# Attention in a two-layer hybrid encoder: the scores of three pairs of heads change their slot

## The chip, the cores and the metric

One core of a Trainium2 chip runs the whole program. The metric is device time in microseconds of one execution. The kernel before took 1118.52 us (median of 3 runs, 1117.92 to 1119.52). All times below come from these runs or from the trace of one profiled execution.

## The reference

Input x is 256 tokens by 1024 channels in float32. Each of two layers does

```
x = LN(alpha*x + 0.5*SwiGLU_1(x))
x = LN(alpha*x + HybridMixer(x))
x = LN(alpha*x + 0.5*SwiGLU_2(x))
```

The mixer multiplies x by one combined input matrix. Its columns feed a state-space branch (u), an indexer (idx), attention (q, k, v; 8 heads of 64) and two gates (gs, ga). The state-space branch is a complex diagonal recurrence per group of 16 channels, then GELU and a gated linear unit. The attention branch lets each query keep its 64 best keys as scored by the indexer, adds a relative-position bias, takes a softmax and multiplies by v:

```
logits = q @ k * HEAD_DIM**-0.5 + bias[bucket(key - query)]   (selected keys only)
p = softmax(logits); out = p @ v
merged = sigmoid(g_ssm)*(y_ssm @ w_branch[0]) + sigmoid(g_attn)*(y_attn @ w_branch[1])
return merged @ w_out
```

## The kernel before, in words

Every weight arrives in tiles of 128 partitions by up to 1024 columns. SyncE loads a tile into a ring of four raw buffers, ScalarE rounds it into a high part (`whi`, `split_hi`, L430), VectorE subtracts to get the low part (`wlo`, `split_lo`, L1246), and TensorE multiplies three times (high by high, high by low, low by high: L744 to L746). A raw buffer is free once its tile is split, so each load waits for the split of four tiles earlier. Each of the five engines runs its own instruction list in order; the lists meet only through semaphores.

In the mixer TensorE runs nine projections c = 0 to 8, each for two token tiles t, each in four quarters q of two contraction tiles (six matmuls a quarter at 512 columns). Small work of the other branches is hooked in after a quarter. Attention is hooked into projections 6 to 8; the quarters there are slots j = 8*(c-6) + 4*t + q, from 0 to 23. The weights of a projection's quarter q are one tile; tiles 20 to 23 belong to projection 7, tiles 24 to 27 to projection 8, tiles 28 and 29 to the gated linear unit, and tiles 30 to 33 to the product after it (counted as in `splits(s + n)`).

The heads go in four pairs p. A pair passes through these steps:

- `att_scores` (TensorE, L1038, 64 rows of the array each): q times k on top of a mask that lies in banks 4 and 2 of PSUM. For pairs 1 to 3 ScalarE has to have put the mask there (`set_masks`, L594).
- `att_logits` (VectorE, L1457): adds the bias, writes `prob` and the negative maximum. From pair 1 on it also waits until the transposes of the pair before have read `prob`.
- `exp_probs` (ScalarE, L584), `invert` (VectorE, L1466), `normalize` (ScalarE, L612).
- `prob_transpose` (TensorE, L1049): turns the probabilities. It waits for `normalize` and for `ya_lo` of the pair before.
- `prt_read` (ScalarE, L602): copies them to SBUF.
- `att_values` (TensorE, L1059, 64 columns of the array each): multiplies by v.
- `ya_hi` (ScalarE, L617) and `ya_lo` (VectorE, L1470): split the output into two parts.

In the same slots the state-space branch has `ssm_out` (TensorE, L999 and L1004), `ssm_turn` and `ssm_scan` (VectorE, L1398 to L1413) and `rotate_back` (GpSimd, L1840 and following). ScalarE also reads the gate projections out of PSUM (`proj_read`, L520). The order in each engine's list is written by hand as a loop over j with tables of slots. Before the change scores stand at slots 3, 7, 11, 15, transposes at 7, 11, 15, 19, values at 8, 12, 16 and 22; in a shared slot the scores come first. `ssm_out` 1 to 3 stand after slots 1, 12 and 17.

VectorE's list from slot 7 on reads: logits of pair 1, split of tile 23, `invert` 1, `ya_lo` 0, `ssm_turn` 3, `ssm_scan` 3, logits of pair 2, split 24, `invert` 2, split 25, `ya_lo` 1, logits of pair 3, split 26, `invert` 3, `ya_lo` 2, split 27. ScalarE's list after the exponentials of pair 1 reads: `ya_hi` 0, `normalize` 1, masks, `proj_read(6,1)`, split 24.

Of the kernel before, what the change touches and what calls it, by code (L numbers as in the profile page):

```python
# [73 lines left out]
TURN_AT = [(1, 1, 1), (2, 0, 1)]  # L74
TURNED = {2: 0, 3: 6}
IDX_AT = [(2, 1, 1), (2, 1, 3), (3, 0, 2)]
OUT_AT = [(5, 1, 1), (6, 0, 1), (7, 1, 1), (8, 0, 1)]
ATT_C = 6
SCORES_AT, TRANSPOSE_AT, VALUES_AT = 3, 7, 8
LAST_VALUES_AT = 22  # L80
GATE_TILES = {1: 22, 2: 23, 8: 24, 13: 27, 16: 28, 17: 29, 18: 30, 20: 31, 21: 32, 22: 33, 23: 34}
READ_AT = {4: (6, 0), 8: (6, 1), 12: (7, 0), 17: (7, 1), 20: (8, 0), 23: (8, 1)}
SLOTS = 8 * (NPROJ - ATT_C)
LAST_K = 3
# [6 lines left out]
N_PAIRS = N_HEADS // 2  # L91
# [10 lines left out]
def build(nc, A, out):  # L102
# [217 lines left out]
    with block:  # L320
# [102 lines left out]
        def _(act):  # L423
# [191 lines left out]
            def ya_hi(l, p):  # L615
                act.wait_ge(S["pv_done"], N_PAIRS * l + p + 1)
                nc.scalar.copy(ya_h[:, p, :], ps[:, PV, 0:SEQ]).then_inc(S["yah_done"], 1)  # L617
# [5 lines left out]
            def mixer(l):  # L623
# [35 lines left out]
                    nc.scalar.copy(y_h[:, cols, :], u_t[:, cols, :]).then_inc(S["yh_done"], 1)  # L659

                for j in range(SLOTS):
                    p, rest = divmod(j - TRANSPOSE_AT, 4)
                    if rest == 0 and 0 <= p < N_PAIRS:
                        prt_read(l, p)
                    if j == 11:
                        splits(s + 25, 2)
                    p, rest = divmod(j - SCORES_AT, 4)
                    if rest == 0 and 0 <= p < N_PAIRS:
                        exp_probs(l, p)
                    if rest == 1 and 1 <= p < N_PAIRS:  # L670
                        ya_hi(l, p - 1)
                    if j == LAST_VALUES_AT:
                        ya_hi(l, N_PAIRS - 1)
                    if rest == 1 and 0 <= p < N_PAIRS:
                        normalize(l, p)
                        if p + 1 < N_PAIRS:
                            set_masks()
                        else:
                            load_table(ACT.Gelu_apprx_tanh)
                    if j in READ_AT:  # L680
                        proj_read(l, *READ_AT[j])
                    if j in GATE_TILES:
                        splits(s + GATE_TILES[j], 1)
                    if j == 18:
                        gelu(0)
                        gelu(1)
                splits(s + 35, 1)
# [53 lines left out]
        def _(pe):  # L741
# [319 lines left out]
                ins.then_inc(S["pv_done"], 1)  # L1061

            def attention(l, j):
                p, last = divmod(j - SCORES_AT, 4)
                if last == 0 and 0 <= p < N_PAIRS:
                    att_scores(l, p)
                p, last = divmod(j - TRANSPOSE_AT, 4)
                if last == 0 and 0 <= p < N_PAIRS:
                    prob_transpose(l, p)
                p, last = divmod(j - VALUES_AT, 4)  # L1070
                if j == LAST_VALUES_AT:
                    att_values(l, N_PAIRS - 1)
                if last == 0 and 0 <= p < N_PAIRS - 1:
                    att_values(l, p)

            def hooks(l, c, t, q):

                for n, where in enumerate(TURN_AT):
                    if (c, t, q) == where:
                        proj_transpose(l, n)  # L1080
                for half, where in enumerate(PAIR_IN):
                    if (c, t, q) == where:
                        ssm_in(l, half)
                for n, where in enumerate(IDX_AT):
                    if (c, t, q) == where:
                        idx_scores(l, n)
                for n, where in enumerate(OUT_AT):
                    if (c, t, q) == where:
                        ssm_out(l, n)
                j = 8 * (c - ATT_C) + 4 * t + q  # L1090
                if j >= 0:
                    attention(l, j)

            def gate_product(l):

# [124 lines left out]
            for l in range(DEPTH):  # L1220
# [4 lines left out]
                last = l + 1 == DEPTH  # L1225
# [3 lines left out]
        def _(dve):  # L1229
# [243 lines left out]
            def mixer(l):  # L1473
# [24 lines left out]
                                                   op0=ALU.add, op1=ALU.mult).then_inc(S["bra_read"], 1)  # L1498

                for j in range(SLOTS):  # L1500
                    p, rest = divmod(j - SCORES_AT, 4)
                    if j == 0:
                        ssm_turn(l, 2)
                    if j == 2:
                        ssm_scan(l, 2)
                    if rest == 0 and 0 <= p < N_PAIRS:
                        att_logits(l, p)
                    if j == 3:
                        splits(s + 20, 1)
                        invert(l, 0)  # L1510
                        splits(s + 21, 2)
                    if j == 7:
                        splits(s + 23, 1)
                        invert(l, 1)
                        ya_lo(l, 0)
                        ssm_turn(l, 3)
                    if j == 10:
                        ssm_scan(l, 3)
                    if j == 11:
                        splits(s + 24, 1)  # L1520
                        invert(l, 2)
                        splits(s + 25, 1)
                        ya_lo(l, 1)
                    if j == 15:
                        splits(s + 26, 1)
                        invert(l, 3)
                        ya_lo(l, 2)
                        splits(s + 27, 1)
# [415 lines left out]
```

## Time and profile before

| what | value |
|---|---|
| median of 3 runs | 1118.52 us |
| lowest and highest | 1117.92 and 1119.52 us |
| span of the profiled execution | 1117.5 us |
| TensorE busy | 1105.8 us, 99% |
| VectorE busy | 752.0 us, 67% |
| ScalarE busy | 561.1 us, 50% |
| GpSimd busy | 391.1 us, 35% |
| granted clock of TensorE, mean | 0.999 |

The profiled execution gives a span from its first to its last instruction, 1117.5 us; what lies around that span is seen only as the difference to the runs, 1.0 us to their median. Matmuls overlap by a pipeline, so that one of 0.39 us starts every 0.23 us; distances between starts are more telling than durations. The attention slots of the first layer lie at about 272 to 320 us of the span, those of the second at about 825 to 872 us.

### The profile page before, as it was taken

The page shows a single profiled execution, that of the slowest core. Times are in us where ns is not written, and L with a number is a line of the kernel's source. Part 1 is how long each engine was busy: PE and PEld are TensorE (multiplying, and loading weights), DVE is VectorE, ACT ScalarE, POOL GpSimd, SP SyncE. Part 2 cuts the span into 40 slices and gives each one's busy share as a digit, 9 for nine tenths or more (in the row PEclk, how much of TensorE's full clock was granted, in tenths as well). Part 3 has the DMA queues.
Part 4 walks back from the last instruction along what each step waited for, and adds up shares of the span by engine and source line. Part 5 has one row for each costly group of instructions (what it writes and reads, how often), then busy time and mean ns, then how long its engine had stood idle before and what let it go on. Part 6 is the DMA issues. An engine that isn't in the chain of part 4 may idle for free.

```text
span 1117.5 us, 17726 instructions
## 1 busy us (share of the span) xinstructions
PE 1105.8 (99%) x5979; PEld 917.9 (82%) x5979; DVE 752.0 (67%) x1073; ACT 561.1 (50%) x805; POOL 391.1 (35%) x560
## 2 busy tenths in 40 slices
PE   9999999999999999999999999999999999999997
PEld 7788888997788888888888888889877888888886
DVE  6657755789977865675575555467898787565544
ACT  6545433674873554543344544336748645453540
POOL 4889975107700188998500000011275000000001
PEclk9999999999999999999999999999999999999999
DMA  9776753644565577565367575536535666657541
GB/s 287 242 228 208 247 176 113 211 136 137 157 223 192 166 224 242 184 221 187 112 201 227 159 245 192 192 91 226 164 112 160 209 199 210 211 172 241 189 150 38
DMA packets 158655, 208.95 MB, mean 187 GB/s; under 512 B 12760, under 2 KB 107128, under 8 KB 158592
## 3 DMA queue, kind: packets, MB, share of 16 engines
q1 hardware_dynamic: 155232, 202.29, 56.7%
q10 hardware_dynamic: 2592, 3.67, 1.2%
q0 software_dynamic: 768, 2.17, 0.6%
q8 instruction: 37, 0.61, 0.2%
q14 instruction: 26, 0.21, 0.1%
HBM read 207.02 MB, written 1.06 MB: 186 GB/s over the span
## 4 chain that ended last, share of the span: by engine, by line
PE 82%; DVE 8%; ACT 3%; issue 3%; DMA 2%; SPq 1%; POOLq 0%; POOL 0%; DVEq 0%; ACTq 0%
PE ps L744 25%; PE ps L746 25%; PE ps L745 25%; DVE wlo L1246 4%; PE ps L768 2%; DMA raw<-in_ffn_w_up 1%; DVE score L1441 1%; ACT whi L430 1%; DMA raw<-in_w_in 1%; PE ps L758 1%; PE ps L986 1%; DVE gates L1413 1%; PE ps L1123 1%; PE ps L1125 1%; PE ps L1126 1%
## 5 line engine op out<-in xcount | busy, mean ns | idle before, releaser
L1246 DVE TENSOR_TENSOR wlo<-raw,whi 128x1024 fp32r<-128x1024 f32 (+1 forms) x371 | 475.7, 1298 | 188.4 <-ACT whi L430 174.2
L430 ACT CAST whi<-raw 128x1024 fp32r<-128x1024 f32 (+1 forms) x371 | 384.7, 1044 | 287.1 <-PE ps L746 225.2
L744 PE MATMUL ps<-whi,xh 128*128 128x512 f32 x976 | 384.4, 394 | 0.2 <-DVE wlo L1246 0.2
L746 PE MATMUL ps<-whi,xl 128*128 128x512 f32 x976 | 377.8, 387 | 0.0
L745 PE MATMUL ps<-wlo,xh 128*128 128x512 f32 x976 | 377.4, 387 | 0.0
L744 PEld LDWEIGHTS ps<-whi,xh 128*128 128x128 f32 x976 | 183.3, 188 | 39.0 <-issue 3.4
L746 PEld LDWEIGHTS ps<-whi,xl 128*128 128x128 f32 x976 | 183.2, 188 | 37.8
L745 PEld LDWEIGHTS ps<-wlo,xh 128*128 128x128 f32 x976 | 183.5, 188 | 34.9
L1671 POOL TENSOR_TENSOR rstd<-var_eps,cst 128x1 f32<-128x1 f32 x12 | 18.2, 1518 | 529.8 <-DVE var_eps L1295 520.7
L744 PE MATMUL ps<-whi,hh 128*128 128x512 f32 (+1 forms) x355 | 139.5, 393 | 0.0
L746 PE MATMUL ps<-whi,hl 128*128 128x512 f32 (+1 forms) x355 | 137.7, 388 | 0.0
L745 PE MATMUL ps<-wlo,hh 128*128 128x512 f32 (+1 forms) x355 | 137.6, 388 | 0.0
L1274 DVE SCALAR_TENSOR_TENSOR h<-silu,ps 128x256 f32<-128x256 f32 x88 | 36.4, 416 | 97.6 <-ACT silu L453 97.6
L453 ACT ACTIVATE silu<-ps 128x256 f32<-128x256 f32 x88 | 33.0, 379 | 134.9 <-PE ps L746 134.8
L746 PEld LDWEIGHTS ps<-whi,hl 128*128 128x128 f32 x355 | 66.7, 188 | 13.9
L744 PEld LDWEIGHTS ps<-whi,hh 128*128 128x128 f32 x355 | 66.7, 188 | 13.5
L745 PEld LDWEIGHTS ps<-wlo,hh 128*128 128x128 f32 x355 | 66.7, 188 | 13.1
L1840 POOL TENSOR_TENSOR h_st<-tab_c,gates 128x512 f32<-128x512 f32 x8 | 10.3, 1294 | 115.3 <-DVE wlo L1246 88.6
L1647 POOL TENSOR_TENSOR small<-small 128x16 f32<-128x16 f32 x102 | 38.2, 375 | 8.5 <-ACT small L464 0.7
L1123 PE MATMUL ps<-xh,whi 128*128 128x256 f32 x128 | 37.4, 292 | 0.0
L1125 PE MATMUL ps<-xl,whi 128*128 128x256 f32 x128 | 36.2, 283 | 0.0
L1126 PE MATMUL ps<-xh,wlo 128*128 128x256 f32 x128 | 36.1, 282 | 0.0
(195 smaller groups left out, 1209.3 us busy)
## 6 DMA issues: line engine op xcount, KB each, us to landing
raw<-in_ffn_w_up SPq DMA_DIRECT2D x351, 256.0 KB, 4.0
raw<-in_ffn_w_down SPq DMA_DIRECT2D x176, 256.0 KB, 3.1
raw<-in_w_in SPq DMA_DIRECT2D x128, 256.0 KB, 3.4
raw<-in_w_branch SPq DMA_DIRECT2D x32, 256.0 KB, 3.3
raw<-in_w_out SPq DMA_DIRECT2D x32, 256.0 KB, 3.8
bias_g<-bias_rows ACTq DMA_DIRECT2D x16, 192.0 KB, 3.7
raw<-in_w_in SPq DMA_DIRECT2D x16, 148.0 KB, 2.3
affine<-in_ln_g SPq DMA_DIRECT2D x4, 512.0 KB, 5.6
```

The costliest lines, as they stand in the source:

```text
L430: nc.scalar.copy(whi[:, s % RING, 0:w], raw[:, s % RAW, 0:w]).then_inc(S["hi_done"], 1)
L453: nc.scalar.activation(silu[:, t, :], ps[:, 2 * b + t, 0:CW], ACT.Silu).then_inc(S["silu_done"], 1)
L744: nc.tensor.matmul(o, ah, bh, start=start, stop=False)
L745: nc.tensor.matmul(o, ah, bl, start=False, stop=False)
L746: return nc.tensor.matmul(o, al, bh, start=False, stop=stop)
L768: ins = nc.tensor.transpose(ps[:, 4 + b, k * SEQ + i * P:k * SEQ + (i + 1) * P], h[:, b, i, k * P:(k + 1) * P], ident[:, :])
L1123: nc.tensor.matmul(o, hi, xh[:, k, :], start=k == 0 and m % 2 == 0, stop=False, skip_group_check=True)
L1125: nc.tensor.matmul(o, hi, xl[:, k, :], start=False, stop=False, skip_group_check=True)
L1126: ins = nc.tensor.matmul(o, lo, xh[:, k, :], start=False, stop=k == KT - 1, skip_group_check=True)
L1246: nc.vector.tensor_tensor(wlo[:, s % RING, 0:w], raw[:, s % RAW, 0:w], f32(whi[:, s % RING, 0:w]), ALU.subtract).then_inc(S["split_done"], 1)
L1274: nc.vector.scalar_tensor_tensor(out=h[:, b, t, :], in0=silu[:, t, :], scalar=0.5, in1=ps[:, 2 * b + t, CW:2 * CW], op0=ALU.mult, op1=ALU. ...
L1647: ins = nc.gpsimd.tensor_tensor(o, a, b, f)
```

## The change

Scores of pairs 1 to 3 move from slots 7, 11, 15 to slots 8, 12, 16, where they come behind the values of the pair before. Transposes and values keep their slots. `ssm_out` 1 moves from slot 1 to slot 3 and `ssm_out` 2 stays at slot 12 but behind the scores there, since attention is now issued ahead of `ssm_out` in a slot. On ScalarE the exponentials of pairs 1 to 3 move to slots 8, 12, 16 and what follows them (`ya_hi`, `normalize`, masks) to slots 9, 13, 17; reads and weight splits that belong to slots 8, 12 and 16 thereby come between the exponentials and `normalize`. The last `prt_read` moves ahead of the two GELUs, and split 30 behind them. VectorE's order stays the same.

```diff
-OUT_AT = [(5, 1, 1), (6, 0, 1), (7, 1, 1), (8, 0, 1)]
+OUT_AT = [(5, 1, 1), (6, 0, 3), (7, 1, 0), (8, 0, 1)]
-SCORES_AT, TRANSPOSE_AT, VALUES_AT = 3, 7, 8
-LAST_VALUES_AT = 22
-GATE_TILES = {1: 22, 2: 23, 8: 24, 13: 27, 16: 28, 17: 29, 18: 30, 20: 31, 21: 32, 22: 33, 23: 34}
+SCORES_AT = {3: 0, 8: 1, 12: 2, 16: 3}
+TRANSPOSE_AT = {7: 0, 11: 1, 15: 2, 19: 3}
+VALUES_AT = {8: 0, 12: 1, 16: 2, 22: 3}
+GATE_TILES = {1: 22, 2: 23, 8: 24, 13: 27, 16: 28, 17: 29, 19: 30, 20: 31, 21: 32, 22: 33, 23: 34}
...
                 for j in range(SLOTS):
-                    p, rest = divmod(j - TRANSPOSE_AT, 4)
-                    if rest == 0 and 0 <= p < N_PAIRS:
-                        prt_read(l, p)
+                    if j in TRANSPOSE_AT and j < 19:
+                        prt_read(l, TRANSPOSE_AT[j])
                     if j == 11:
                         splits(s + 25, 2)
...
+                    if j in SCORES_AT:
+                        exp_probs(l, SCORES_AT[j])
+                    if j - 1 in SCORES_AT:
+                        p = SCORES_AT[j - 1]
+                        if p > 0:
+                            ya_hi(l, p - 1)
                         normalize(l, p)
...
                     if j in READ_AT:
                         proj_read(l, *READ_AT[j])
                     if j in GATE_TILES:
                         splits(s + GATE_TILES[j], 1)
                     if j == 18:
+                        prt_read(l, N_PAIRS - 1)
                         gelu(0)
                         gelu(1)
...
             def attention(l, j):
...
+                if j in TRANSPOSE_AT:
+                    prob_transpose(l, TRANSPOSE_AT[j])
+                if j in VALUES_AT:
+                    att_values(l, VALUES_AT[j])
+                if j in SCORES_AT:
+                    att_scores(l, SCORES_AT[j])
...
+                j = 8 * (c - ATT_C) + 4 * t + q
+                if j >= 0:
+                    attention(l, j)
                 for n, where in enumerate(OUT_AT):
                     if (c, t, q) == where:
                         ssm_out(l, n)
-                j = 8 * (c - ATT_C) + 4 * t + q
-                if j >= 0:
-                    attention(l, j)
```

## Rows read from the trace of the kernel before

**Rows 1.** The page: busy time, and the chain that ended last.
```profile
PE 1105.8 (99%) x5979; PEld 917.9 (82%) x5979; DVE 752.0 (67%) x1073; ACT 561.1 (50%) x805; POOL 391.1 (35%) x560
...
PE 82%; DVE 8%; ACT 3%; issue 3%; DMA 2%; SPq 1%; POOLq 0%; POOL 0%; DVEq 0%; ACTq 0%
```

**Rows 2.** Waits in 262 to 330 us: who waited for whom, us, times, longest.
```profile
PEld ps L1038 <- ACT ps L594: 1.4, 1, 1.4
```

**Rows 3.** Timeline, TensorE, slots 7 and 8, first layer (start, duration, then the idle time before).
```profile
285.40 0.93 PE L1038 MATMUL ps<-k_t,q_t 64*128 64x128 f32 x8 [1.01 <-ACT ps L594]
...
289.25 0.50 PE L744 MATMUL ps<-whi,xh 128*128 128x512 f32 x1
```

**Rows 4.** Timeline, TensorE, slots 11 and 12, first layer.
```profile
293.23 0.39 PE L746 MATMUL ps<-whi,xl 128*128 128x512 f32 x1
293.55 0.93 PE L1038 MATMUL ps<-k_t,q_t 64*128 64x128 f32 x8
294.41 0.87 PE L1049 MATMUL ps<-ident,prob 128*128 128x128 f32 x6
295.04 0.47 PE L744 MATMUL ps<-whi,xh 128*128 128x512 f32 x1
...
296.60 0.87 PE L1059 MATMUL ps<-prob_t,v_sb 128*64 128x256 f32 x8
297.40 0.50 PE L744 MATMUL ps<-whi,xh 128*128 128x512 f32 x1
```

**Rows 5.** Timeline, TensorE: `ssm_out` 2, last transposes and last values, first layer.
```profile
299.21 1.08 PE L1004 MATMUL ps<-h_st,c_t 128*32 128x128 f32 x32
...
312.74 0.82 PE L1049 MATMUL ps<-ident,prob 128*128 128x128 f32 x6
...
318.03 0.87 PE L1059 MATMUL ps<-prob_t,v_sb 128*64 128x256 f32 x8 [0.37 <-ACT prob_t L602]
```

**Rows 6.** Timeline, ScalarE, pairs 0 and 1, first layer.
```profile
283.07 1.50 ACT L612 ACTIVATE prob<-prob,inv_sum 128x128 f32<-128x128 f32 x4 [0.24 <-DVE inv_sum L1466]
...
287.98 0.40 ACT L584 ACTIVATE prob<-prob,neg_max 128x128 f32<-128x128 f32 x1
...
289.76 0.35 ACT L617 CAST ya_h<-ps 128x256 fp32r<-128x256 f32 x1
290.75 1.50 ACT L612 ACTIVATE prob<-prob,inv_sum 128x128 f32<-128x128 f32 x4 [0.65 <-DVE inv_sum L1466]
...
292.97 0.58 ACT L520 ACTIVATE gates<-ps 128x512 f32<-128x512 f32 x1
293.46 1.03 ACT L430 CAST whi<-raw 128x1024 fp32r<-128x1024 f32 x1
```

**Rows 7.** Timeline, VectorE, pairs 1 to 3, first layer.
```profile
287.30 0.29 DVE L1457 CUSTOM_DVE_ANT_0 prob<-ps,bias_g 128x128 f32<-128x128 f32 x1
...
288.44 2.19 DVE L1246 TENSOR_TENSOR wlo<-raw,whi 128x1024 fp32r<-128x1024 f32 x1
...
295.38 2.34 DVE L1413 TENSOR_TENSOR_SCAN gates<-decay,gates 128x512 f32<-128x512 f32 x2
...
302.33 0.41 DVE L1470 TENSOR_TENSOR ya_l<-ps,ya_h 128x256 fp32r<-128x256 f32 x1
...
308.72 1.21 DVE L1246 TENSOR_TENSOR wlo<-raw,whi 128x1024 fp32r<-128x1024 f32 x1
```

**Rows 8.** Timeline, VectorE and GpSimd, 288 to 293 us, first layer.
```profile
289.62 2.06 POOL L1647 TENSOR_TENSOR h_st<-h_st,h_tmp 128x512 f32<-128x512 f32 x1
...
290.95 1.82 DVE L1398 TENSOR_TENSOR h_st<-gates,tab_s 128x1024 f32<-128x1024 f32 x1
```

**Rows 9.** Timeline, TensorE, slots 7 and 11, second layer.
```profile
837.00 0.93 PE L1038 MATMUL ps<-k_t,q_t 64*128 64x128 f32 x8 [0.18 <-ACT ps L594]
...
846.04 0.87 PE L1049 MATMUL ps<-ident,prob 128*128 128x128 f32 x6
```

**Rows 10.** Busy time by engine in 277 to 330 us; the 1.00 is the granted clock.
```profile
277.00:330.00 53.00, 51.61 (x347) 39.99 (x346) 45.65 (x93) 43.59 (x98) 20.30 (x12) 1.00 0.60 185
```

More of the change, by code:

```diff
@@ L661, in mixer @@
                 for j in range(SLOTS):
-                    p, rest = divmod(j - TRANSPOSE_AT, 4)
-                    if rest == 0 and 0 <= p < N_PAIRS:
-                        prt_read(l, p)
+                    if j in TRANSPOSE_AT and j < 19:
+                        prt_read(l, TRANSPOSE_AT[j])
                     if j == 11:
                         splits(s + 25, 2)
[L667 to L674, printed above, removed]
+                    if j in SCORES_AT:
[4 more added lines that the diff above has]
+                            ya_hi(l, p - 1)
                         normalize(l, p)
@@ L679, in mixer @@
                             load_table(ACT.Gelu_apprx_tanh)
+                    if j == 22:
+                        ya_hi(l, N_PAIRS - 1)
                     if j in READ_AT:
@@ L1063, in attention @@
             def attention(l, j):
[L1064 to L1074, printed above, removed]
+                if j in TRANSPOSE_AT:
[4 more added lines that the diff above has]
+                    att_scores(l, SCORES_AT[j])
             def hooks(l, c, t, q):
@@ L1500, in mixer @@
                 for j in range(SLOTS):
-                    p, rest = divmod(j - SCORES_AT, 4)
                     if j == 0:
@@ L1505, in mixer @@
                         ssm_scan(l, 2)
-                    if rest == 0 and 0 <= p < N_PAIRS:
-                        att_logits(l, p)
+                    if j == 10:
+                        ssm_scan(l, 3)
+                    if j in SCORES_AT:
+                        att_logits(l, SCORES_AT[j])
                     if j == 3:
@@ L1511, in mixer @@
                         splits(s + 21, 2)
-                    if j == 7:
+                    if j == 8:
                         splits(s + 23, 1)
@@ L1516, in mixer @@
                         ssm_turn(l, 3)
-                    if j == 10:
-                        ssm_scan(l, 3)
-                    if j == 11:
+                    if j == 12:
                         splits(s + 24, 1)
@@ L1523, in mixer @@
                         ya_lo(l, 1)
-                    if j == 15:
+                    if j == 16:
                         splits(s + 26, 1)
```

## The prediction, made before the run

> **What bounds the kernel now.** I read the page first: TensorE is busy for 1105.8 of 1117.5 us, and the chain that ended last runs over it for 82% [rows 1]. A change pays only if TensorE issues less or waits less, and it costs what TensorE then waits. So I next read the waits of the attention stage. TensorE's largest is for the masks ahead of pair 1's scores, 1.4 us before the weight load [rows 2]. Then the busy time of that stage: of 53 us TensorE works 51.6, VectorE 45.7, ScalarE 43.6 [rows 10]. The helpers are 82 to 86% busy, so a delayed step there can't catch up within a slot or two. Last I read the timeline engine by engine, by distances between starts.
>
> **TensorE's own work.** In slots 11 and 12 the last projection matmul is followed by scores 0.32 us later, transposes after another 0.86, the projection after 0.63 [rows 4]. Six projection matmuls and the step to the values take 1.56, the values 0.80 [rows 4]. Eighteen projection matmuls from the end of slot 8 to the scores take 293.55 - 289.25 = 4.30 [rows 3, 4]; to transposes I take 4.2.
> Moving scores behind the values removes one change of array shape a pair: before 128 rows, 64 rows, 128 rows, and again 64 columns, 128; after it only 64 columns, 64 rows, 128. The step into a 64-row group costs 0.32 against the usual 0.23, and the first projection matmul after a visit costs another 0.1 (the durations 0.47 and 0.50 against 0.39 show it) [rows 4]. I take 0.15 for each of three pairs and 0.1 for each of the two `ssm_out` visits that now share a slot with scores: 0.65 a layer, 1.3 in all. Bounds: 0 (the step costs as much in its new place) to 2.0 (0.2 for each of ten).
> The Trainium skill, page "TensorEngine Tiling (Array Packing)", Key Properties, says that changing the tiling mode drains TensorE. The extra 0.1 us of rows 4 agrees with that; by this rule alone the change would be a gain of about 1 us (my estimate from the row), and the rest of the sum would have to come from waits.
>
> **What goes.** Pair 1's scores no longer wait for masks: 1.0 us in the first layer [rows 3], 0.2 in the second [rows 9]. In the first layer the transposes of pair 0 take over part of the wait, for `normalize` ends at 283.07 + 1.50 = 284.57 [rows 6], while TensorE is there at about 284.2. `prt_read` ahead of the GELUs removes the wait of the last values, 0.4 a layer [rows 5].
>
> **What comes: pair 1.** I write the first layer's new schedule with the old durations.
> Transposes 0 start at 284.6, the projection at 285.2, values 0 at 286.8, scores 1 at 287.6, the projection at 288.45. Before it was 289.25 with the same work done [rows 3]: TensorE is 0.8 ahead.
> Scores 1 end 0.93 after their start, at 288.5; logits 1 start at 288.65, against 287.30 before [rows 7]. So the pair starts 1.35 later, though TensorE is earlier: the logits used to start when slot 7's transposes had ended, now behind slot 8's scores. The exponentials start 0.7 later and last 289.76 - 287.98 = 1.8 [rows 6]: done at 291.1.
> Now ScalarE's new order. `proj_read(6,1)` takes 0.5 and split 24 about 1.0 [rows 6]; both used to follow `normalize`, now they stand ahead. Then `ya_hi` 0.35 and `normalize` 1.5 [rows 6]: 291.1 + 0.5 + 1.0 + 0.35 + 1.5 = 294.45.
> TensorE could turn these probabilities at 288.45 + 4.2 = 292.65. It starts at 294.5, 1.85 late. (Inside this lies an earlier wait: split 23 is queued behind the logits on VectorE, 289.85 plus 2.1 is 291.95 [rows 7], and the projection wants that tile at 291.3.) The former transposes 1 started at 294.41 [rows 4], but had 0.86 of scores behind them.
> What is queued behind on VectorE: `ya_lo` 0 waits for the late `ya_hi`, until 293.0, and `ssm_turn` 3, `ssm_scan` 3 and all that follows stand behind it.
>
> The 2.1 of split 23 is a 1.2 us operation [rows 7] that waited for GpSimd; GpSimd's next operation in turn took 2.06, and the next of VectorE 1.82 [rows 8]. The Trainium skill, page "SBUF — State Buffer", gives the reason: VectorE and GpSimd share a port pair that is locked for the whole instruction. By the lock, split 23 would again start behind a GpSimd operation and end at 291.95; without it, at 291.05, and this would change nothing in the sum, since `normalize` is later than both.
>
> **Pair 2.** Projection from 295.1, values 1 at 296.65, scores 2 at 297.5, `ssm_out` 2 from 298.3 for 1.4 [rows 5], projection from 299.7; transposes 2 could start at 303.9. VectorE: `ya_lo` 0 until 293.3, `ssm_turn` 3 takes 3.85 (4.4 before, less 0.6 of GpSimd's), the scan starts at 297.15. From the scan's start to `ya_lo` 1 it took 302.33 - 295.38 = 6.95, plus 0.4 [rows 7]; VectorE has no gap there, so it is done at 304.5, and the transposes wait for it: 0.65. (`normalize` 2 ends at 304.2, just under it.)
>
> **Pair 3.** Projection from 305.2, values 2 at 306.8, scores 3 at 307.6, projection from 308.5, `ssm_out` 3 at 310.0, slot 18 from 311.35, slot 19's quarter wanted at 312.85. The exponentials start at 309.4 and end at 311.15. Split 28 now stands behind them on ScalarE (1.0), then `ya_hi` 2 (0.35); only then VectorE can do `ya_lo` 2 (0.3) and, behind it, split 27 (1.2), which slot 19's quarter needs: 314.05. TensorE waits 1.25. Transposes 3 start at 315.5, against 312.74 before [rows 5], all earlier work being equal: 2.75 behind.
> The last values don't wait: 0.4 back. **First layer: +2.3 to +2.4.**
>
> **Second layer.** The same steps, but TensorE arrived later relative to the helpers there: the mask wait was 0.2, not 1.0 [rows 9], so there is less to regain at slot 7 (0.5 instead of 0.8). Transposes 1 come at 846.4 against 846.04 [rows 9]; the same working puts the end 0.3 further behind: **+2.6**.
>
> **Behind the slots** TensorE waited for nothing that now is late enough: the GELUs end 2.9 later, but `y_split` still precedes the gate product by 1.8, and the last `ya_lo`, delayed 3.1, comes 2 us ahead of the branch product. At nothing, then; if that cover goes, up to 1 us a layer.
>
> **Sum.** 2.3 + 2.6 = +4.9 us on a profiled span of 1117.5; the median of the runs is 1.0 above that span, and I carry this over: 1118.5 + 4.9 = **1123.4 us**. Bounds of the sum: the waits of pair 1 and 3 are differences of two long chains, each good to 0.5 us, four of them: +2.9 to +6.9.
>
> **Rivals.**
> A. The helpers keep up and the kernel gets faster. For it: `normalize` 1 ended at 290.75 + 1.50 = 292.25 [rows 6], 2.15 before its transposes [rows 4]. Then only what goes counts: 1.3 of shapes, 1.2 of mask waits less 0.4 for pair 0, 0.8 of last values: -2.9, 1115.6 us. Against it: the new transposes are due at 292.65, so any delay of `normalize` 1 over 0.4 us decides against A, and the pair starts 1.35 later with 1.5 of ScalarE's work put ahead of `normalize`; only 0.65 of this can fall into the wait for `invert` that stood there [rows 6].
> B. The delays hit only one pair (pair 1), VectorE catching up in its idle 2.3 us before logits 3. Then each layer has pair 1's 1.85, less 0.8 at slot 7, 0.4 at the last values and 0.15 for shapes at pairs 2 and 3: +0.5 a layer, 1119.5 us. Against it: pair 3's wait comes from split 28 ahead of `ya_hi` 2 in ScalarE's list, not from a backlog.
> C. The lag of the helpers (3 to 3.6 us) reaches the gate and branch products, because raw loads wait for late splits: +8, 1126.5 us. Against: 2 us of cover.
>
> **Chances.** Forecast 0.63 (own range 1121.4 to 1125.4), A 0.12, B 0.13, C 0.12. For 8 in 10 I leave A out and part of C: 1118.8 to 1126.3. A measurement of this kernel can tell about 0.2% (2.2 us) from no change, not less. Faster: A, 0.12. Within 0.2%: nearly all of B, 0.12. Slower: 0.76.
>
> **What would show it.** In the new trace: scores 1 without a wait behind values 0, the projection resuming 0.8 earlier than at 289.25 (first layer); TensorE waiting about 1 us or more for ScalarE's `normalize` ahead of transposes 1; about 0.7 ahead of transposes 2, the releaser being VectorE's `ya_lo`; about 1.2 for `wlo` in front of slot 19's quarter; no wait ahead of the last values. TensorE's idle time grows by some 6 us in all. I am wrong if `normalize` 1 ends before TensorE gets to transposes 1, or if the granted clock, 1.00 throughout this stage [rows 10], moves.

## The result, and the profile after

The changed kernel takes 1125.02 us (median of 4 runs, 1124.22 to 1125.11). Run beside it, the kernel before took 1118.89 us (4 runs, 1117.92 to 1119.52). The ratio is 1.0054 with a 95% interval from 1.004 to 1.0068: slower by 6.1 us. The forecast was 1123.4 us with a range of 1118.8 to 1126.3, so the measured time lies inside the range, 1.6 us above the forecast.

The profiled execution took 1125.09 us, 1.8 us more than its span; the span grew by 5.8 us, from 1117.5 to 1123.3. TensorE's busy time is the same within 0.7 us, and what grew is its idle time, from 1117.5 - 1105.8 = 11.7 us [rows 1] to 1123.3 - 1106.5 = 16.8 us. The page of after:

```profile
span 1123.3 us, 17726 instructions
...
PE 1106.5 (99%) x5979; PEld 918.1 (82%) x5979; DVE 747.9 (67%) x1073; ACT 561.3 (50%) x805; POOL 391.9 (35%) x560
```

The chain of waits is no help this time: as followed back in this trace it covers only 22% of the span. The better view is TensorE's waits over the whole kernel (who waits <- who releases it: us, times, longest):

```profile
PE ps L1050 <- ACT prob L613: 2.8, 2, 1.4
PE ps L745 <- DVE wlo L1242: 2.1, 2, 1.0
PE ps L769 <- DVE h L1270: 1.6, 1, 1.6
...
PE ps L1050 <- DVE ya_l L1466: 1.3, 2, 0.6
PE ps L745 <- ACT gates L521: 0.4, 1, 0.4
```

Three of these come "2 times", once a layer, and are new: transposes for `normalize`, a projection quarter for `wlo`, transposes for `ya_lo`. The mask wait [rows 2] and the last values' wait [rows 5] are gone. The wait of L769 lies at 29.8 us, in the first feed-forward block, which the change doesn't touch: it was 0.7 us in the trace of before, 1.6 here, and 1.7 in a second execution of before. Here the new waits stand in the first layer (timeline of TensorE in after; most lines have moved by one). One thing must be known to read it: TensorE's matmuls overlap, and the idle time in brackets counts from the modelled end of the one before, so a wait of 1.42 moves the start by more. By starts, transposes 1 come 295.06 - 293.25 = 1.81 us after the last matmul ahead of them, where 0.23 is the step without a wait: 1.58 us late. In the same way transposes 2 are 0.78 late, and slot 19's quarter 1.19.

```profile
284.69 0.87 PE L1050 MATMUL ps<-ident,prob 128*128 128x128 f32 x6
286.00 0.50 PE L745 MATMUL ps<-whi,xh 128*128 128x512 f32 x1 [0.44 <-ACT gates L521]
287.59 0.87 PE L1060 MATMUL ps<-prob_t,v_sb 128*64 128x256 f32 x8
288.39 0.93 PE L1039 MATMUL ps<-k_t,q_t 64*128 64x128 f32 x8
...
293.25 0.39 PE L747 MATMUL ps<-whi,xl 128*128 128x512 f32 x1
295.06 0.87 PE L1050 MATMUL ps<-ident,prob 128*128 128x128 f32 x6 [1.42 <-ACT prob L613]
...
305.33 0.85 PE L1050 MATMUL ps<-ident,prob 128*128 128x128 f32 x6 [0.62 <-DVE ya_l L1466]
...
314.67 0.50 PE L745 MATMUL ps<-whi,xh 128*128 128x512 f32 x1 [1.03 <-DVE wlo L1242]
316.16 0.82 PE L1050 MATMUL ps<-ident,prob 128*128 128x128 f32 x6
...
321.02 0.87 PE L1060 MATMUL ps<-prob_t,v_sb 128*64 128x256 f32 x8
323.33 0.28 PE L745 MATMUL ps<-y_hl,whi 128*128 128x256 f32 x1
```

Transposes 3 start at 316.16, against 312.74 before, and the last values at 321.02 instead of 318.03 [rows 5], now without a wait. In the second layer the same waits stand in the same places:

```profile
849.43 0.87 PE L1050 MATMUL ps<-ident,prob 128*128 128x128 f32 x6 [1.37 <-ACT prob L613]
...
869.05 0.50 PE L745 MATMUL ps<-whi,xh 128*128 128x512 f32 x1 [1.03 <-DVE wlo L1242]
```

ScalarE's list shows why `normalize` 1 is late (timeline of ScalarE in after, first layer):

```profile
284.54 0.88 ACT L595 CAST ps<-mask 128x384 f32<-128x384 bf16 x2
285.36 0.59 ACT L521 ACTIVATE gates<-ps 128x512 f32<-128x512 f32 x1
...
290.06 0.41 ACT L585 ACTIVATE prob<-prob,neg_max 128x128 f32<-128x128 f32 x1 [3.36 <-DVE neg_max L1453]
...
291.83 0.58 ACT L521 ACTIVATE gates<-ps 128x512 f32<-128x512 f32 x1
292.31 1.04 ACT L431 CAST whi<-raw 128x1024 fp32r<-128x1024 f32 x1
293.25 0.36 ACT L618 CAST ya_h<-ps 128x256 fp32r<-128x256 f32 x1
293.51 1.50 ACT L613 ACTIVATE prob<-prob,inv_sum 128x128 f32<-128x128 f32 x4
```

It begins at 293.51, 2.76 behind the 290.75 of before [rows 6]. The exponentials begin 2.1 later than before (290.06 against 287.98), and behind them a gate read and a split stand ahead of it. The stage has no more work, only more pauses, as far as a fixed window can show it (busy time by engine in 277 to 330 us of after, as in rows 10):

```profile
277.00:330.00 53.00, 49.47 (x362) 37.94 (x359) 39.94 (x87) 39.40 (x92) 19.41 (x12) 1.00 0.54 159
```

TensorE works 2.1 us less of these 53 than in [rows 10], at the same granted clock of 1.00. Part of the difference on the other engines is only that their work comes later and leaves the window.

One detail of the change reads differently in the code than in the text ahead: `ssm_out` 2 doesn't stay at slot 12. Its entry in `OUT_AT` is (7, 1, 1) before, which is slot 8 + 4 + 1 = 13, and (7, 1, 0) after, slot 12, behind the values and scores there. So two `ssm_out` visits of a layer change their slot.

**The yardstick for the experiments.** One section holds all that the change touches: from the first projection matmul of projection 6 to the first matmul of the gate product (323.33 above). I read its two ends off the timeline of each trace:

| kernel | first layer | second layer | span | ratio of the runs to before |
|---|---|---|---|---|
| before | 49.91 | 49.07 | 1117.5 | |
| before, another execution | 49.21 | 48.87 | 1116.8 | |
| after | 52.62 | 51.85 | 1123.3 | 1.0054 [1.004, 1.0068] |
| e2, scores moved alone | 52.36 | 52.36 | 1123.3 | 1.0052 [1.0037, 1.0067] |
| e3, splits behind `normalize` | 51.51 | 50.87 | 1121.6 | 1.003 [1.0017, 1.0042] |
| e7, gate read ahead of masks | 51.66 | 51.63 | 1122.3 | 1.0045 [1.0029, 1.006] |
| e8, splits and gate read rearranged | 49.74 | 49.75 | 1117.7 | 1.001 [1.0001, 1.0018] |
| e9, e8 with `ya_lo` 1 first | 49.55 | 49.59 | 1117.5 | 1.0014 [1.0005, 1.0023] |
| e10, ScalarE's order in before | 48.87 | 49.32 | 1116.8 | 1.0002 [0.9992, 1.0011] |
| e1, last read early in before | 49.42 | 48.39 | 1116.4 | 0.9995 [0.9985, 1.0005] |
| e4, transposes ahead of scores in before | 48.65 | 48.67 | 1116.0 | 0.9994 [0.9985, 1.0003] |
| e5, e1 and e4 | 49.40 | 48.61 | 1116.8 | 0.9989 [0.998, 0.9997] |
| e6, `ssm_out` moved in before | 49.24 | 48.84 | 1116.5 | single run |

### The profile page after: what moved, and what is told of

The parts are those of the page before. It is cut to its first block and busy times, and to the rows that moved or that the text cites. A ratio compares the mean times of both kernels' runs of the same rounds, so it can differ in the third digit from the quotient of the medians.

```text
span 1123.3 us, 17726 instructions
## 1 busy us (share of the span) xinstructions
PE 1106.5 (99%) x5979; PEld 918.1 (82%) x5979; DVE 747.9 (67%) x1073; ACT 561.3 (50%) x805; POOL 391.9 (35%) x560
```

## The experiments

**Another execution of the kernel before** (b2), for what one trace can tell.

> The kernel before, unchanged, profiled once more. In the traces so far the scan ahead of logits 0 in the first layer started between 277.3 and 278.3 us of the span, while TensorE's place varied by 0.2. My reading: VectorE's phase against TensorE at the start of the attention slots differs from one execution to the next (the first layer's mask wait was 1.0 us here, 0.4 in the kernel with ssm_out moved), so that a first-layer difference under 0.5 us between two single traces means nothing, while the second layer's holds to 0.2. Expected: first layer's mask wait between 0.4 and 1.1 us, second layer's slots within 0.2 us of the first trace of before. Rival (the phase is a property of each kernel's order): 1.0 us again, scan at 278.0.

Nothing is changed. It ran once, in 1118.65 us. The first layer's mask wait, 1.01 in [rows 3], is 0.27 here, a little below what was expected, and the section is 0.70 us shorter in the first layer and 0.20 in the second (TensorE's timeline, then VectorE's scan and the logits of pair 0 behind it, in b2):

```profile
285.04 0.93 PE L1038 MATMUL ps<-k_t,q_t 64*128 64x128 f32 x8 [0.27 <-ACT ps L594]
```
```profile
277.64 2.34 DVE L1413 TENSOR_TENSOR_SCAN gates<-decay,gates 128x512 f32<-128x512 f32 x2
279.91 0.29 DVE L1457 CUSTOM_DVE_ANT_0 prob<-ps,bias_g 128x128 f32<-128x128 f32 x1
```

The scan starts at 278.01 in the trace of before, 0.37 us later than here, while TensorE's scores of pair 0 start 0.38 earlier there (277.80 against 278.18): the place of the helpers against TensorE shifts by 0.75 us from one execution to the next, and the mask wait with it. By these two executions a first-layer section is good to 0.7 us, a second-layer one to 0.2; two executions are few, and the experiments below have to be read with this in mind. Against the mean of both executions of before, the change costs 3.06 and 2.88 us.

**Scores moved alone** (e2): the changed kernel with `ssm_out` and the last read as before.

```diff
-OUT_AT = [(5, 1, 1), (6, 0, 3), (7, 1, 0), (8, 0, 1)]
+OUT_AT = [(5, 1, 1), (6, 0, 1), (7, 1, 1), (8, 0, 1)]
...
-                    if j in TRANSPOSE_AT and j < 19:
+                    if j in TRANSPOSE_AT:
...
-                        prt_read(l, N_PAIRS - 1)
...
```

(Left out: split 30 goes back ahead of the GELUs, and `ssm_out` is again issued ahead of attention in a slot.)

> The changed kernel with two parts undone: ssm_out back to its old slots and ahead of attention in a slot, the last prt_read behind the GELUs and split 30 ahead of them. What is left is the move of the scores with ScalarE's steps. My theory: this part carries more than the whole loss; 0.4 to 0.5 us a layer comes back as a wait of the last values and 0.1 to 0.2 for two more visits of ssm_out, so about 1.2 us above the changed kernel's span of 1123.3, 1124.5. Rival (the loss comes from moving ssm_out behind scores, or from the reordered end): the span falls by 1 us or more, to 1122 or less.

The ratio is that of the full change, so the move of the scores, with ScalarE's steps, carries all of its loss. The further 1.2 us that was expected on top didn't come: the span is 1123.3, as in after. In the second layer the section is 0.51 longer than after's, most of which is the wait at the last values come back. In the first it is 0.26 shorter in spite of that wait: the gate read holds slot 8's projection by 0.2 us here (the step from the transposes to it is 0.78 us, against 0.57 without a wait), and by 0.74 in after (1.31). In the second layer the two are alike, 0.20 and 0.22 (TensorE's waits, whole kernel, then three rows of its timeline, in e2):

```profile
PE ps L1049 <- ACT prob L613: 2.7, 2, 1.4
PE ps L744 <- DVE wlo L1241: 2.1, 2, 1.0
...
PE ps L1049 <- DVE ya_l L1465: 1.1, 2, 0.6
PE ps L1059 <- ACT prob_t L603: 0.8, 2, 0.4
```
```profile
288.26 0.50 PE L744 MATMUL ps<-whi,xh 128*128 128x512 f32 x1
...
294.07 0.88 PE L1049 MATMUL ps<-ident,prob 128*128 128x128 f32 x6 [1.37 <-ACT prob L613]
...
320.50 0.87 PE L1059 MATMUL ps<-prob_t,v_sb 128*64 128x256 f32 x8 [0.38 <-ACT prob_t L603]
```

The projection resumes at 288.26, which is the head start of 0.8 that the prediction reckoned with, and it is lost all the same.

**Splits 24 and 28 behind `normalize`** (e3), in the changed kernel.

```diff
-GATE_TILES = {1: 22, 2: 23, 8: 24, 13: 27, 16: 28, 17: 29, 19: 30, 20: 31, 21: 32, 22: 33, 23: 34}
+GATE_TILES = {1: 22, 2: 23, 13: 27, 17: 29, 19: 30, 20: 31, 21: 32, 22: 33, 23: 34}
...
                         normalize(l, p)
+                        if p in (1, 3):
+                            splits(s + (24 if p == 1 else 28), 1)
```

> The changed kernel with only ScalarE's list touched: splits 24 and 28 stand behind normalize 1 and 3 (and the masks or the table load) and no longer ahead of ya_hi. TensorE's list is untouched. My theory: normalize 1 ends 1.0 us earlier (transposes 1 of the first layer at 294.1 where they were at 295.06), ya_lo 0 and with it pair 2 come 1.0 us earlier, and the wait of 1.0 us for wlo in front of slot 19's quarter goes: -2.1 us a layer, span 1119.1. Rival 1 (scores behind values cost TensorE itself more: array shapes, visits): no change, 1123.3. Rival 2 (the pair only starts too late, and what stands ahead of normalize is hidden behind invert): at most -0.5 us a layer, 1122.3 or more.

It gained 1.1 and 1.0 us a layer, about half of what was expected. The wait for `normalize` 1 fell from 1.42 to 0.46, that of the projection quarter for `wlo` is gone, so both splits were causes. But new waits came up, for `prt_read` 1 (0.25) and for a gate read at slot 19 (0.53), which took back part of the gain (timeline of TensorE in e3):

```profile
297.05 0.87 PE L1062 MATMUL ps<-prob_t,v_sb 128*64 128x256 f32 x8 [0.25 <-ACT prob_t L603]
304.80 0.85 PE L1052 MATMUL ps<-ident,prob 128*128 128x128 f32 x6 [0.29 <-DVE ya_l L1468]
...
316.03 0.50 PE L747 MATMUL ps<-whi,xh 128*128 128x512 f32 x1 [0.53 <-ACT gates L521]
```

Split 24 now delays `prt_read` 1, and split 28 the gate read after it: 1 us put behind one deadline stands ahead of the next.

**The gate read of projection 6 ahead of the masks** (e7), in the changed kernel. The projection of slot 8 rewrites the PSUM bank that `proj_read(6,0)` reads, and that read stood behind `normalize` 0 and the masks.

```diff
-READ_AT = {4: (6, 0), 8: (6, 1), 12: (7, 0), 17: (7, 1), 20: (8, 0), 23: (8, 1)}
+READ_AT = {8: (6, 1), 12: (7, 0), 17: (7, 1), 20: (8, 0), 23: (8, 1)}
...
                         normalize(l, p)
+                        if p == 0:
+                            proj_read(l, 6, 0)
```

> The changed kernel with one step moved in ScalarE's list: proj_read(6,0) stands between normalize 0 and the masks, not behind the masks. It tests the wait that my prediction left out (the projection of slot 8 waits until ScalarE has read bank 0). My theory: slot 8's quarter no longer waits (0.7 us in the first layer, 0.2 in the second), everything up to transposes 1 comes that much earlier since the pair's chain starts from scores 1: -0.6 to -0.9 us, span 1122.5. Rival (transposes 1 are bound by ScalarE's work from earlier on, not by scores 1): the time moves into the wait ahead of transposes 1, span 1123.3.

The wait at slot 8 is gone; the section lost 0.96 us in the first layer, 0.22 in the second, and the span 1.0, as expected. The runs, 1.0045 [1.0029, 1.006], can't tell e7 from after. The trace of after itself gives 0.74 and 0.22 us: TensorE is held from about 285.3 to 286.0 in the first layer. This is the one wait of after that the prediction hadn't.

**Three pieces of ScalarE's work rearranged** (e8): e7, with split 24 behind `prt_read` 1 and split 28 behind the gate read (7,1); scores stay in their new slots. This is not quite the order of before: the reads (6,1) and (7,0) still stand ahead of `normalize`, and the read (6,0) stands earlier than it ever did.

```diff
-GATE_TILES = {1: 22, 2: 23, 8: 24, 13: 27, 16: 28, 17: 29, 19: 30, 20: 31, 21: 32, 22: 33, 23: 34}
+GATE_TILES = {1: 22, 2: 23, 13: 27, 17: 29, 19: 30, 20: 31, 21: 32, 22: 33, 23: 34}
...
                     if j == 11:
-                        splits(s + 25, 2)
+                        splits(s + 24, 3)
...
                         proj_read(l, *READ_AT[j])
                     if j in GATE_TILES:
+                        if j == 17:
+                            splits(s + 28, 1)
```

> The changed kernel with ScalarE's list put in order for it: proj_read(6,0) between normalize 0 and the masks, split 24 behind the prt_read of pair 1, split 28 behind proj_read(7,1). TensorE's and VectorE's lists stay as changed. My theory: of the 2.7 us a layer that the change costs, the run with the splits behind normalize showed 1.1 to belong to the splits; the reads put back 0.4 to 0.5 more and the last one 0.5; some 0.6 to 0.8 us a layer stay, because pair 1's scores start only behind slot 8's values: span 1119.0. Rival (with ScalarE's order mended the change pays, through its fewer waits): 1116.5 or less.

4.6 of the 6 us come back (1125.02 against 1120.43), a little more than the 4.3 expected. The second layer's section stays 0.7 us longer than that of before, as expected; the first layer's lies between the two executions of before. What is left of waits in the first layer's slots, in TensorE's timeline of e8:

```profile
292.52 0.87 PE L1054 MATMUL ps<-ident,prob 128*128 128x128 f32 x6 [0.25 <-ACT prob L613]
...
302.80 0.84 PE L1054 MATMUL ps<-ident,prob 128*128 128x128 f32 x6 [0.62 <-DVE ya_l L1470]
```

**`ya_lo` 1 ahead of split 25 on VectorE** (e9), in e8.

```diff
                         invert(l, 2)
-                        splits(s + 25, 1)
                         ya_lo(l, 1)
+                        splits(s + 25, 1)
```

> The mended version of the changed kernel (ScalarE's list in order) with one more swap, in VectorE's list: ya_lo 1 stands ahead of split 25. It tests the term of pair 2: transposes 2 waited 0.6 us a layer for ya_lo 1. My theory: ya_lo 1 comes 2 us earlier, the wait goes, normalize 2 is ready within 0.2 us of need: -0.5 us a layer against the mended version (section of the second layer +0.7 becomes +0.2 against before), span about 1116.7. Rival (normalize 2 is the true bound, as it was just under ya_lo in the prediction's working): -0.2 us a layer or less.

The wait for `ya_lo` went, as e8's trace said it should, but the sections are only 0.19 and 0.16 us shorter, so the rival that was named (0.2 us a layer or less) held, and the runs show nothing of it. Other waits were close behind (TensorE's waits in e9, whole kernel):

```profile
PE ps L749 <- DVE wlo L1246: 0.6, 2, 0.4
PE ps L1064 <- ACT prob_t L603: 0.5, 2, 0.2
```

**ScalarE's order alone** (e10): the kernel before, scores in their old slots, with the gate reads and the splits 24 and 28 ahead of `normalize`.

```diff
-GATE_TILES = {1: 22, 2: 23, 8: 24, 13: 27, 16: 28, 17: 29, 18: 30, 20: 31, 21: 32, 22: 33, 23: 34}
-READ_AT = {4: (6, 0), 8: (6, 1), 12: (7, 0), 17: (7, 1), 20: (8, 0), 23: (8, 1)}
+GATE_TILES = {1: 22, 2: 23, 7: 24, 13: 27, 15: 28, 17: 29, 18: 30, 20: 31, 21: 32, 22: 33, 23: 34}
+READ_AT = {4: (6, 0), 7: (6, 1), 11: (7, 0), 17: (7, 1), 20: (8, 0), 23: (8, 1)}
```

> The kernel before with only ScalarE's order of the changed kernel: proj_read(6,1) and split 24, proj_read(7,0), and split 28 stand between the exponentials and normalize of pairs 1, 2 and 3; scores stay at slots 7, 11 and 15. It fills the last corner of a square: slots moved or not, work ahead of normalize or not. My theory (each alone fits into the 2.1 us that normalize 1 had to spare, only both together don't): normalize 1 ends 0.85 us later, at 293.1 of the first layer, still 1.3 ahead of its transposes; ya_lo 2 and split 27 come 0.8 later and still 0.9 ahead of slot 19's quarter: sections of the two layers within 0.3 us of the kernel before (49.2 to 49.9 and 48.9 to 49.1), span 1116.5 to 1117.5. Rival (ScalarE's order alone carries the loss that mending it gave back): +2 us a layer, 1121.

The runs show no cost. The trace has one in the second layer, a wait of 0.61 us for the masks ahead of pair 2's scores, and a section 0.25 us longer than in the profiled before. Most of the loss is thus an interaction: ScalarE's order without the move costs 0.02% (e10, interval over zero), the move with ScalarE's list rearranged 0.1% (e8), the two as in after 0.54%. The comparison isn't a clean square, since e8 also takes away the wait for the read (6,0), 1.0 us of span by e7, and leaves two reads ahead of `normalize`; the scores moved with ScalarE's list exactly as in before was not run.

The spare time of `normalize` 1 explains it. In before it ended at 292.25 and its transposes began at 294.41, 2.16 later [rows 4, 6]. ScalarE's order alone fits in there: in e10 `normalize` 1 starts 3.45 us after the exponentials (290.53 and 287.08), 0.68 more than in before. The move uses it up nearly by itself: it makes the pair later and the transposes due earlier, and in e8 they still start 0.4 us late by starts (first layer) and 0.1 (second). From there on every further delay of `normalize` 1 is paid.

**The small parts.** e1 is the kernel before with `prt_read` 3 ahead of the GELUs and split 30 behind them; e6 the kernel before with the `ssm_out` visits of after; e4 and e5 go the other way: the kernel before with the transposes ahead of the scores in slots 7, 11 and 15, alone and with e1.

```diff
 e1:                if j == 18:
+                        prt_read(l, N_PAIRS - 1)
                         gelu(0)
                      (and the old prt_read 3 taken out, split 30 to slot 19)
 e4: -                if last == 0 and 0 <= p < N_PAIRS:
     -                    att_scores(l, p)
                      (prob_transpose and att_values, unchanged)
     +                if last == 0 and 0 <= p < N_PAIRS:
     +                    att_scores(l, p)
 e6: -OUT_AT = [(5, 1, 1), (6, 0, 1), (7, 1, 1), (8, 0, 1)]
     +OUT_AT = [(5, 1, 1), (6, 0, 3), (7, 1, 0), (8, 0, 1)]
                      (and attention issued ahead of ssm_out in a slot)
```

> The kernel before with one part of the change alone: the last prt_read stands ahead of the GELUs and split 30 behind them. My theory (TensorE pays only where it waits for a helper's list): the wait of the last values (0.4 us in each layer) goes and nothing else moves, -0.8 us on the span (1117.5 to about 1116.7). Rival (the GELUs, now 0.75 us later, are needed by the gate product or by split 30): 0 or up to +1 us.

> The kernel before with only the ssm_out moves: ssm_out 1 behind the scores of slot 3, ssm_out 2 behind the values of slot 12. My prediction priced sharing a slot at -0.1 us a visit, 0.4 in all. What the changed kernel's trace suggests instead: the step from scores to ssm_out's full-width product takes 0.1 us longer than from the projection, which eats the visit saved: 0 within 0.2 us. A rival for the loss of the change (ssm_out in the new slots makes VectorE's ssm_turn or GpSimd late): +0.5 us a layer or more.

> The kernel before with one thing changed: in the shared slots 7, 11 and 15 the transposes stand ahead of the scores. Scores keep their slots and ScalarE's list is untouched. My theory (a late wait downstream takes back what is gained upstream): transposes 0 start when normalize 0 is done, the mask wait of scores 1 falls away (0.9 us in the first layer, 0.2 to 0.3 in the second), but the last values wait for prt_read behind the GELUs, which does not depend on TensorE's pace, so their wait grows by the same amount: the span stays within 0.3 us of 1117.5. Rival (what TensorE gains early it keeps): -1.2 us, 1116.3.

> The kernel before with the transposes ahead of the scores in slots 7, 11 and 15 and the last prt_read ahead of the GELUs. My theory: now nothing takes the early gain back; 0.5 us a layer at the last values, 0.9 and 0.3 at the masks: -2.0 us, span 1115.5, the fastest version of this study. Rival (the two gains overlap, since the last values are late for another reason): the span of the early prt_read alone, 1116.4.

e1: the wait at the last values is gone, and the section is shorter by 0.5 to 0.7 us in the second layer; 0.9995 [0.9985, 1.0005] is too small for the runs to show. e6: within 0.03 us of one or the other execution of before, so the shared `ssm_out` visit saves nothing that a section shows. e4 was expected to give all back at the last values and didn't: the section is 0.2 to 1.3 us shorter, though the runs, 0.9994 [0.9985, 1.0003], leave zero open.

The step of e4's expectation that failed is that the last `prt_read` doesn't depend on TensorE's pace. With the transposes ahead of the scores, `prt_read` 2 no longer keeps ScalarE from the exponentials of pair 3, and ScalarE's list behind them runs with hardly a gap down to `prt_read` 3. In the second layer both start 1.4 us earlier in the trace (ScalarE in e4, then in before), of which 1.0 is the earlier start of the whole section:

```profile
855.95 0.40 ACT L584 ACTIVATE prob<-prob,neg_max 128x128 f32<-128x128 f32 x1 [0.70 <-DVE neg_max L1457]
...
867.28 0.86 ACT L602 COPY prob_t<-ps 128x384 f32<-128x384 f32 x2
```
```profile
857.39 0.40 ACT L584 ACTIVATE prob<-prob,neg_max 128x128 f32<-128x128 f32 x1
...
868.73 0.85 ACT L602 COPY prob_t<-ps 128x384 f32<-128x384 f32 x2
```

In the first layer the exponentials start 0.96 us earlier (304.79 against 305.75), and `prt_read` 3 starts 1.62 earlier (315.50 against 317.12). The other 0.65 is `normalize` 3's wait for `invert` 3, which is gone there because split 26 ahead of it on VectorE is shorter. With `prt_read` 3 that early the last values hardly wait in either layer (VectorE's split and GpSimd's operation beside it; first e4, then before):

```profile
305.24 1.36 DVE L1246 TENSOR_TENSOR wlo<-raw,whi 128x1024 fp32r<-128x1024 f32 x1
```
```profile
305.60 2.06 POOL L1647 TENSOR_TENSOR h_st<-h_st,h_tmp 128x512 f32<-128x512 f32 x1
```
```profile
306.21 2.19 DVE L1246 TENSOR_TENSOR wlo<-raw,whi 128x1024 fp32r<-128x1024 f32 x1
```
```profile
306.14 1.18 POOL L1647 TENSOR_TENSOR h_st<-h_st,h_tmp 128x512 f32<-128x512 f32 x1
```

In e4 the split goes first and GpSimd is the slow one, in before it is the other way round. This flip is in the first layer alone: in e4's second layer the split took 2.15 us and GpSimd's operation 1.19, as in before.

e5 is the fastest kernel of this study, 0.9989 [0.998, 0.9997] (1118.03 us). That is 0.1% below the kernel before, with an interval that only just leaves out zero gain, and half of the 2 us that were expected; the early read adds nothing that the runs can tell from e4.

## Why the prediction was right, point by point

**What bounds the kernel, and the direction.** Right. TensorE's busy time stayed (1105.8 and 1106.5 us); the loss is waits. Its idle time grew by 5.1 us, where the prediction said some 6.

**Pair 1.** Right, and tested. Expected: scores without a wait, `normalize` done at 294.45, transposes at 294.5 after a wait of 1.85. Measured: scores without a wait, `normalize` done at 293.51 + 1.50 = 295.01, transposes at 295.06, 1.58 late by starts, which is how the prediction reckons. `normalize` was done 0.56 later than reckoned, and TensorE was there 0.83 later (293.48 against 292.65), which is the missing term below. Split 23 took 1.43 us, not the 2.1 that the prediction carried over from [rows 7] (VectorE's timeline of after):

```profile
290.51 1.43 DVE L1242 TENSOR_TENSOR wlo<-raw,whi 128x1024 fp32r<-128x1024 f32 x1
```

GpSimd's operation ran from 289.66 to 290.85 and overlapped it by 0.34 us; the split took 0.2 more than an undisturbed one (1.22 us at 310.40). The Trainium skill, page "SBUF — State Buffer", section "SBUF: two separate sides", lets the one wait for the other's whole instruction: the trace agrees, for the split ended 1.09 us after GpSimd's operation here, and 1.08 after it for split 26 in before (308.40 and 307.32). The price depends on when each comes. As reckoned, it changed nothing in the sum.

**Pair 2.** Right: 0.65 expected for `ya_lo` 1, 0.78 measured by starts (0.62 of idle time). e9 removed this wait by the one edit that its reason names.

**Pair 3.** Right in place, cause and size: 1.25 expected in front of slot 19's quarter, 1.19 measured by starts in the first layer (1.03 of idle time in both). The order that makes it can be read from VectorE in after: `ya_lo` 2 waits for `ya_hi`, and split 27, the first of the two below, stands behind it.

```profile
313.06 0.42 DVE L1466 TENSOR_TENSOR ya_l<-ps,ya_h 128x256 fp32r<-128x256 f32 x1 [1.03 <-ACT ya_h L618]
313.40 2.35 DVE L1242 TENSOR_TENSOR wlo<-raw,whi 128x1024 fp32r<-128x1024 f32 x2
```

e3 took split 28 away from ahead of `ya_hi`, and the wait went.

**The term that was missing.** The prediction let the projection resume 0.8 earlier, at 288.45. In after it resumed where it had before, at about 289.25, since the projection of slot 8 first waited for `proj_read(6,0)` to empty its bank. In before, the scores of pair 1 stood there, with their wait for the masks, and took up this time. So part of what the prediction counted as regained, the mask wait, only changed its name. The price is 0.74 and 0.22 us by the trace of after, 0.96 and 0.22 by e7; the first layer's value changes from one execution to the next like the mask wait did, for in e2 it is 0.2, and the projection resumes at 288.26.

**TensorE's own work.** The term is 0.4 us too large. The prediction took 0.1 us for each of two `ssm_out` visits that share a slot, 0.2 a layer. In e6 and in after nothing of it is seen. From the last projection matmul ahead to the second one behind, `ssm_out` takes 1.90 us by itself and scores with their mask 1.85; together they take 3.29, and the two projection steps that the second visit would have covered (0.46) are all the difference. Coming from the scores, the first matmul of the visit is followed by the second line's matmuls 0.42 us later (slot 3 of after), against 0.32 where it comes from the projection, as in e2 (299.41 and 299.73); the saved change of shape is paid one step further on:

```profile
277.50 0.49 PE L1000 MATMUL ps<-u_t,k_t 128*128 128x128 f32 x2
277.92 1.08 PE L1005 MATMUL ps<-h_st,c_t 128*32 128x128 f32 x32
```

The other 0.15 for each of three pairs is right, as the traces show without a run of its own. Measured in the same way, a pair takes 2.12 (scores and transposes) + 1.47 (values) = 3.59 us in before, and 1.12 (transposes) + 2.32 (values and scores) = 3.44 in the new order, read where TensorE doesn't wait for the transposes (pair 3's in after, pair 0's in e7 and e8). Where it waits, as for pairs 1 and 2 in after, the saving drowns in the wait. The 0.4 did not enter the forecast, whose schedule gives this visit 1.4 us (1.44 measured); it counts in rival A's sum. The rule cited from the Trainium skill, page "TensorEngine Tiling (Array Packing)", Key Properties, that a change of mode drains TensorE, is not contradicted: it says that a switch costs, and what failed was my count of the switches that would go.

**The last values and the cover behind the slots.** Right: no wait at the last values, and none at the gate and branch products. e1 takes this wait of 0.4 us away in before, and e2 brings it back.

**The sum.** Expected +2.35 and +2.6. Measured section against the profiled before: 52.62 - 49.91 = +2.71 and 51.85 - 49.07 = +2.78, together 5.5; the other 0.3 of the span's 5.8 lies outside the sections, where the wait at 29.8 us alone differs by 0.9 between these two executions. Where the first layer went off is seen by starts, forecast against measured: transposes 0 284.6 and 284.69, scores 1 287.6 and 288.39, transposes 1 294.5 and 295.06, transposes 2 304.5 and 305.33, transposes 3 315.5 and 316.16. The forecast is 0.8 short at scores 1, which is the gate read, and stays 0.6 to 0.8 short; the steps between, set by the helpers, are each right to 0.3. Of the 0.66 at the end 0.29 drops out of the section, which began at 270.71 and not 270.42. The second layer's 0.2 is the size of its gate read, 0.22. The parts don't add up to a tenth, as e3 and e9 show, and the first layer's sum is no better known than the 0.7 us between two executions.

The sections and what lies outside them make up 5.8 - 4.9 = 0.9 of the 1.7 us between the forecast and the profiled execution (1125.09). The rest, 0.8, is the step from the span to the run time: the prediction added the 1.0 us between the span of one profiled execution and the median of three runs, but in after and in every experiment an execution takes about 1.8 us more than its own span (1125.09 against 1123.3). By this the profiled execution of before took about 1119.3 us, more than the median of its three runs, and 1118.52 was a low median: the 13 to 29 runs of before beside the experiments have medians of 1118.94 to 1119.39 us.

**The rivals.** A (helpers keep up) fell with `normalize` 1, done 1.5 us after TensorE got there. B (only pair 1) fell with the waits of pairs 2 and 3. C (the lag reaches the products) fell with the list of TensorE's waits, which has none for these.

**Left open.** With scores moved and the three pieces of work rearranged, e8 is still slower than before by 0.1%, and e9 doesn't change that. Its logits 1 start 0.5 us later than before (287.79 against 287.30), and which of the small waits behind that makes the 0.1% isn't settled. That GpSimd's and VectorE's order can flip was read from two traces, in one layer of one of them, and not tried by itself.

## What to carry to other kernels

Before moving a step on the bound engine, write for each helper queue by how much each of its results is early: here `normalize` 1 had 2.1 us to spare, enough for more work ahead of it or, all but 0.4 us, for the moved scores, and not for both. Reckon that a moved step does two things to this time: it makes the helper's result later, and it may bring the next use of it nearer. Look at what the moved step used to cover as well: in its old place it hid a wait of the following matmul for a bank to be read. A wait that goes is worth little while the next is 0.2 to 0.5 us behind it, as e9 shows: the splits alone gave 2.2 us (e3), the gate read 0.9 (e7), all three with places that suit them 4.6 (e8).

## What the runs showed of the hardware

- The same VectorE split of 128x1024 took 1.36 or 2.19 us, and GpSimd's operation beside it 2.06 or 1.18, according to which of them started first. Of the 1.6 us by which `prt_read` 3 moved, 0.65 turned on that.
- Between two executions of the same kernel a helper stood 0.37 us earlier (scan at 277.64 and 278.01) and TensorE 0.38 later at the same points of the program, and one wait of TensorE was 1.01 or 0.27 us. By itself, a difference below 0.7 us in the first layer's section of one trace means nothing; the medians of ten to thirty runs just told 0.1% apart.
- In `ssm_out`, from the first full-width matmul to those on 32 columns, starts are 0.42 us apart if the array was at 64 rows (after) or 64 columns (e6, slot 12) just before, and 0.32 behind a projection: what an adjacent visit saved at the projection was paid there.
- A wait costs TensorE more than the idle time that the profile gives: 1.42 us of idle time went with a start 1.58 us late.
